# Split scores for the later tiles of an NSA attention, squares of the memory on GpSimd, and two conv halves ahead

## The reference, cut to what matters

```python
def first_block(...):
    h = hybrid_mixer(rmsnorm(x, norms[l, 0]), ...)
    x = x + rmsnorm(h, norms[l, 1])
    h = memory_attention(rmsnorm(x, norms[l, 2]), rmsnorm(mem, mem_norm[l]), ...)
    x = x + rmsnorm(h, norms[l, 3])
    h = swiglu(rmsnorm(x, norms[l, 4]), ...)
    x = x + rmsnorm(h, norms[l, 5])

def hybrid_mixer(h, w_in, w_out, gn_nsa, gn_conv, ...):
    proj = h @ w_in                       # q, three pairs of k and v, gates, conv parts
    ...
    out = g_c[..., 0:1] * o_cmp + g_c[..., 1:2] * o_sel + g_c[..., 2:3] * o_win
    ...
    merged = jnp.concatenate([rmsnorm(o_nsa, gn_nsa), rmsnorm(o_conv, gn_conv)], axis=-1)
    return merged @ w_out
```

## Time and profile before

| | |
|---|---|
| median of 3 runs | 2499.2 us (2498.59 to 2503.46) |
| the profiled execution | 2500.74 us, its span 2498.7 us |
| TensorE busy | 2454.7 us (98%) |
| VectorE, ScalarE, POOL busy | 1578.5, 965.6, 1289.3 us (63%, 39%, 52%) |
| mean granted clock of TensorE | 0.996 |

### The profile page before, as it was taken

One profiled execution on the slowest core, in us unless ns is written; L12 is line 12 of the kernel. 1 busy time (PEld: TensorE's weight loads), 2 busy tenths in 40 slices (PEclk: granted clock), 3 DMA queues, 4 the chain that ended last, 5 costly groups with the idle time before them and its releaser, 6 DMA issues.

```text
span 2498.7 us, 32840 instructions
## 1 busy us (share of the span) xinstructions
PE 2454.7 (98%) x12363; PEld 2074.6 (83%) x12363; DVE 1578.5 (63%) x2572; ACT 965.6 (39%) x1573; POOL 1289.3 (52%) x671
## 2 busy tenths in 40 slices
PE   9999999999999999999999999999999999999998
PEld 6877766877786777788789999999999888888886
DVE  2246244776402735422379897998940699999995
ACT  3256455222323435523333333434333433333333
POOL 3630322444454433144434887766666567666662
PEclk9999999999999999999999999999999999999999
DMA  5320222655433221022223888999998899999992
GB/s 215 118 68 1 68 68 76 202 197 182 152 101 127 76 85 66 32 98 93 101 81 118 297 298 287 356 354 360 358 322 260 296 363 359 364 367 361 367 363 90
DMA packets 212733, 508.90 MB, mean 204 GB/s; under 512 B 18401, under 2 KB 101345, under 8 KB 212193
## 3 DMA queue, kind: packets, MB, share of 16 engines
q1 hardware_dynamic: 123696, 338.22, 38.6%
q0 software_dynamic: 36864, 134.23, 15.1%
q10 hardware_dynamic: 52016, 34.36, 4.4%
HBM read 454.31 MB, written 52.43 MB: 203 GB/s over the span
## 4 chain that ended last, share of the span: by engine, by line
PE 89%; DVE 3%; POOL 3%; ACT 3%; DMA 1%; issue 1%; ACTq 0%; DVEq 0%; SPq 0%
PE bank L2130 73%; PE bank L2682 3%; PE bank_and L2130 3%; POOL weight_split L807 3%; PE bank L2255 3%; PE bank_and L2098 2%; PE bank L2245 1%; ACT weight_split L948 1%; PE bank_and L2230 1%; DMA ring<-weights 1%; PE bank L2230 1%; PE bank L2109 1%; PE bank_and L2495 0%; PE bank L2554 0%; DVE h_split L1424 0%
## 5 line engine op out<-in xcount | busy, mean ns | idle before, releaser
L2130 PE MATMUL bank<-h_split,weight_split 128*128 128x384 f32 (+1 forms) x5568 | 1133.9, 362 | 12.9 <-POOL weight_split L807 4.9
L2130 PEld LDWEIGHTS bank<-h_split,weight_split 128*128 128x128 f32 x5568 | 994.7, 188 | 126.1 <-POOL weight_split L807 11.9
L807 POOL TENSOR_TENSOR weight_split<-ring,weight_split 128x1024 fp32r<-128x1024 f32 x182 | 452.9, 2488 | 758.4 <-ACT weight_split L948 758.2
L2130 PE MATMUL bank<-late_weight_split,weighted_split 128*128 128x512 f32 x2268 | 514.8, 389 | 0.0
L2130 PEld LDWEIGHTS bank<-late_weight_split,weighted_split 128*128 128x128 f32 x2268 | 425.5, 188 | 88.3
L834 POOL DMA_INDIRECT arena<-weights,arena x256 | 314.2, 1228 | 146.1 <-DVE arena L1884 59.6
L823 POOL TENSOR_TENSOR weight_split<-ring,weight_split 128x1024 fp32r<-128x1024 f32 x129 | 310.3, 2406 | 120.8 <-ACT weight_split L1321 120.1
L948 ACT ACTIVATE weight_split<-ring 128x1024 fp32r<-128x1024 f32 x182 | 192.0, 1055 | 292.2 <-PE bank L2130 276.9
L1321 ACT ACTIVATE weight_split<-ring 128x1024 fp32r<-128x1024 f32 x130 | 137.8, 1061 | 390.2 <-PE bank L2130 336.3
L2026 DVE TENSOR_TENSOR arena<-arena 128x384 f32<-128x384 f32 x128 | 224.8, 1756 | 21.3 <-DMA arena<-expert_acts 20.9
L823 POOL TENSOR_TENSOR late_weight_split<-ring,late_weight_split 128x1024 fp32r<-128x1024 f32 x63 | 152.7, 2424 | 102.8 <-ACT late_weight_split L1321 102.2
(11 more groups left out here) (349 smaller groups left out, 2718.3 us busy)
## 6 DMA issues: line engine op xcount, KB each, us to landing
ring<-weights SPq DMA_DIRECT2D x493, 512.0 KB
expert_acts<-arena SPq DMA_DIRECT2D x128, 192.0 KB
gates_spread<-arena ACTq DMA_DIRECT2D x24, 1024.0 KB
arena<-gates_spread SPq DMA_DIRECT2D x96, 256.0 KB
arena<-expert_acts SPq DMA_DIRECT2D x128, 192.0 KB
arena<-weights,arena POOLq DMA_INDIRECT x256
arena<-bias_sel ACTq DMA_DIRECT2D x1, 2048.0 KB, 7.8
arena<-bias_band ACTq DMA_DIRECT2D x1, 2048.0 KB, 7.8
```

The lines of the kernel that those rows point to most:

```text
L807: nc.gpsimd.tensor_tensor(w_split[:, (count - 1) % 2, 1, :], ring[:, n % RING, :], w_split[:, (count - 1) % 2, 0, :], ALU.subtract).then_i ...
L2130: ins = mm(*args, start=start, stop=stop)
```

## The change

The first block only:

- **Scores of the token tiles 2 and 3, window and selected stage.** Each unit's fp32 matmul becomes two fp32r matmuls: one of depth 128, with the query's high part in the rows of its group and its low part in the other half's rows, against the keys' high part in both halves; and one of depth 64, high query by low key (`score_rest`). The new tiles `late_queries_split`, `keys_high_twice` and `keys_low` lie in the space of `h_split`.
- **Who makes the parts.** POOL casts keys and queries and subtracts the keys' low part, after the token values and ahead of w_out's low parts. VectorE copies the keys' high parts to the other half (behind pair 2 and pair 9) and makes the queries' low parts, two behind each of pairs 3 to 6.
- **Memory.** Its DMA is issued by ScalarE at pair 2 of the window stage. POOL squares and adds the chunks behind its attention parts, and TensorE makes one sum matmul of 128x256 instead of 8. ScalarE takes the root behind the selected stage.
- **w_out.** TensorE makes the conv halves of tiles 0 and 1, then turns the merged output, then makes the merged halves of both.
- **Start.** `small` has its own semaphore, const's DMA stands behind x's chunk 2, TensorE waits for const before the second chunk, VectorE before its first evacuation. Six matmuls on zeros instead of eight.

```diff
+            def key_parts(branch):
+                for g in range(2):
+                    nc.gpsimd.tensor_copy(k_twice[half[g], branch, g, :], qk[half[g], 6 + branch, :]).then_inc(k_high, 1)
+                    pool.wait_ge(k_high, 2 * (1 - branch) + g + 1)
+                for g in range(2):
+                    nc.gpsimd.tensor_tensor(k_low[half[g], branch, :], qk[half[g], 6 + branch, :],
+                                            k_twice[half[g], branch, g, :], ALU.subtract).then_inc(k_lowered, 1)
+                    pool.wait_ge(k_lowered, 2 * (1 - branch) + g + 1)
+            def attention_parts():
+                pool.wait_ge(*taken(first["qk"] + 7))
+                pool.wait_ge(proj_done, first["vtok"] + NT)
+                key_parts(1)
+                for n in range(NH):
+                    g, m = n % 2, n // 2
+                    nc.gpsimd.tensor_copy(q_split[half[g], m + 4 * g, :], qk[half[g], m, 2 * P:T]).then_inc(q_high, 1)
+                    pool.wait_ge(q_high, n + 1)
+                key_parts(0)
...
+                if count == tile_of[first["w_out"]]:
+                    attention_parts()
+                    memory_squares()
...
             for k in range(0, KD, 2):
                 act_e.dma_start(xT[:, k, :], x_in[k]).then_inc(x_loaded[k], 16)
-                if k == 0:
+                if k == 2:
                     act_e.dma_start(const[:, :], consts_in).then_inc(consts_in_sem, 16)
...
                 if pair == 2:
+                    act_e.dma_start(memT, mem_in.rearrange("k p m -> p k m")).then_inc(mem_loaded, 16)
                     weight_high(first["w_out"])
...
+            root(2, D, NM)
...
-            act_e.dma_start(memT, mem_in.rearrange("k p m -> p k m")).then_inc(mem_loaded, 16)
...
-            act_e.wait_ge(mem_loaded, 16)
-            norm(2, lambda k: memT[:, k, :], D, NM)
...
+            def query_low(n):
+                g, m = n % 2, n // 2
+                dve.wait_ge(q_high, n + 1)
+                v.tensor_tensor(q_split[half[1 - g], m + 4 * g, :], qk[half[g], m, 2 * P:T],
+                                q_split[half[g], m + 4 * g, :], ALU.subtract).then_inc(q_low, 1)
+            def attention_parts(pair):
+                if pair == 2:
+                    key_in_other_half(1)
+                if 3 <= pair < 7:
+                    query_low(2 * pair - 6)
+                    query_low(2 * pair - 5)
+                if pair == 9:
+                    key_in_other_half(0)
...
+            def score_rest(u, w, q, k):
+                mm(bank[S_BANK[u % 4]][:, 0:w], q, k, start=False, stop=True).then_inc(qk_done, 1)
...
             def nsa_k(i, branch, lo):
+                if t >= 2:
+                    if branch:
+                        pe.wait_ge(q_low, min(i % (2 * NH) + 1, NH))
+                    pe.wait_ge(k_copied, 2 * (2 - branch))
+                    pe.wait_ge(k_lowered, 2 * (2 - branch))
+                    return k_twice[:, branch, g, lo * P:(t + 1) * P]
```

More of the change, by code:

```diff
@@ L786, in add_square, with memory_squares @@
                 nc.gpsimd.tensor_tensor(sum_, before, sq[:, n % 2, :], ALU.add).then_inc(sq_summed, 1)
+            half = [slice(g * HD, (g + 1) * HD) for g in range(2)]
+            def key_parts(branch):
[15 more added lines that the diff above has]
+                key_parts(0)
+            def memory_squares():
+                pool.wait_ge(mem_loaded, 16)
+                nc.gpsimd.tensor_tensor(mem_acc, memT[:, 0, :], memT[:, 0, :], ALU.mult).then_inc(mem_squared, 1)
+                for k in range(1, KD):
+                    pool.wait_ge(mem_squared, 2 * k - 1)
+                    nc.gpsimd.tensor_tensor(mem_sq, memT[:, k, :], memT[:, k, :], ALU.mult).then_inc(mem_squared, 1)
+                    pool.wait_ge(mem_squared, 2 * k)
+                    last = nc.gpsimd.tensor_tensor(mem_acc, mem_acc, mem_sq, ALU.add)
+                    last.then_inc(mem_squared if k < KD - 1 else sq_ready, 1)
             def add_chunks(n, y):
@@ L1575, in _ @@
             late_rstd(0)
+            dve.wait_ge(consts_in_sem, 16)
             for k in range(8):
@@ L2225, in token_major, with score, scores @@
                     release(1)
-            def score(u, w, q, k):
+            def score(u, w, q, k, last=True):
                 if u >= 4:
                     pe.wait_ge(logits_ready, u - 3)
-                mm(bank[S_BANK[u % 4]][:, 0:w], q, k, start=True, stop=True).then_inc(qk_done, 1)
-            def attend(u0, g0, units, per, q, k, blocks, head, vals, before_turn=None, begun=0, busy=(0, 0),
[L2233 to L2237, removed]
+                ins = mm(bank[S_BANK[u % 4]][:, 0:w], q, k, start=True, stop=last)
+                if last:
+                    ins.then_inc(qk_done, 1)
+            def score_rest(u, w, q, k):
+                mm(bank[S_BANK[u % 4]][:, 0:w], q, k, start=False, stop=True).then_inc(qk_done, 1)
+            def attend(u0, g0, units, per, q, k, blocks, head, vals, before_turn=None, begun=0, busy=(0, 0),
+                       after_turn=None, rest=lambda i: None):
+                def scores(pair):
+                    both = [i for i in (2 * pair, 2 * pair + 1) if i >= begun]
+                    for i in both:
+                        score(u0 + i, P * blocks(i), q(i), k(i), last=rest(i) is None)
+                    for i in both:
+                        if rest(i):
+                            score_rest(u0 + i, P * blocks(i), *rest(i))
                 def turn_prob(i):
@@ L2266, in attend @@
                     if pair < units // 2:
-                        scores(2 * pair)
-                        scores(2 * pair + 1)
+                        scores(pair)
                     if pair == 1 and before_turn and not after_turn:
```

89 lines of the change are left out of this document (65 added, 24 removed).

## The result

The changed kernel took 2505.71 us in the median of 22 runs, the kernel before 2500.91 us in as many: a ratio of 1.0035 (95% interval 1.002 to 1.005), slower by 4.8 us where 2.2 us less had been forecast. The single runs say more than the median. Those of before lie between 2498.59 and 2504.76. Those of the changed kernel lie between 2497.91 and 2523.39: three near 2498, nine between 2501 and 2506, eight between 2519 and 2524, and two in between (2508.22 and 2511.48). Their mean granted clock goes with it: 0.995 to 0.997 for the first three, 0.993 to 0.994 for the nine, 0.984 to 0.987 for the eight, 0.992 and 0.989 for the two. The profiled execution is one of the last eight (2522.53, its span 2520.7), so its trace shows what such a run loses.

What follows compares the result with a forecast made beforehand. TensorE, carrying 89% of the chain that ended last, was taken as the bound; start −1.1, window stage +4.5, selected stage −1.1 and w_out −4.5 gave −2.2 on 2499.2: 2497.0 us, range 2490.5 to 2503.5.

Steps and rivals of the forecast that it cites:

- the clock behind pair 7's pause: Window stage: after a 4 us pause TensorE's granted clock falls, adding 1.2 us (0 to 1.7).
- The pause itself: Window stage, VectorE: pair 7's reductions start at 178.0 instead of 173.91, +4.1 us, TensorE idle nearly all of it.
- The casts: POOL, from the window stage's start: 0.9 us for each 512-wide cast, 0.5 at 256.
- case C: Window stage: POOL casts cost 1.4 and 0.75 us, pair 7's reductions come at 181.8 (+7.9); 2501.3 us, chance 0.20.
- Case B: Window stage: VectorE has room, pair 7 stays near 173.91; −7.2 us, 2492.0, chance 0.26.
- Case D: Pair 7 waits as in case C, 64-row rests run one behind the other; +6.6 us, 2505.8, chance 0.12.
- The scores: TensorE: 384-wide pairs take 0.73 us instead of 0.85, rests side by side; window stage −0.8, selected stage −1.1.
- The start: TensorE's first product starts at 10.6 instead of 11.69: −1.1 us (−0.7 to −1.3), and the gain stays.
- w_out: TensorE gains 6.4 us, gives back 2.0 waiting for POOL's low part of tile 2: −4.5.

Runs made afterwards that it cites:

- late lows: The changed kernel with VectorE's query lows two each behind pairs 3, 4, 7 and 8 instead of 3 to 6; 2494.48 us, ratio 0.998.

## Why the prediction was wrong

**The sign and the size fell with one term, the clock behind pair 7's pause.** The prediction took it from the earlier trace rows, where twelve products behind 1.90 us of idling took 4.58, as "1.2 (0 to 1.7)". There the engine had 512-wide products to run, and the clock was back after some 3 us. In the window stage it has small matmuls (64 values wide, transposes of 128, scores of 384), and the fall lasted up to 50 us: +23.4 where +0.4 stood, in a third of the runs; the middle ones are 3 to 8 us above the best. The step assumed that a fall is over once the engine works again, within some 3 us. I had the warning in view: the stage's stream isn't that of the row from which I took the price.

The other terms, as measured, add up to −1.1 + 3.6 (window scores and pause) − 0.8 (selected stage with the memory's sum) − 4.6 = −2.9, that is 2498.0, where the three best runs lie (2497.9 to 2498.4). The forecast without its 1.2 was −3.4. The median is 7.7 us above 2498.0, where 1.2 stood for the clock, and the granted clock of these middle runs is the lower one (0.993 to 0.994). None of them was profiled, so how much of the 7.7 fell in the window stage stays open.

The Trainium skill ("TensorE: Matmul & The Clock Gate", Part 1) says that the array's clock follows how busy it has been of late. The kernel with matmuls behind the pause agrees (spread 1.6 us instead of 25); but busy in the sense of the profile's rows is not enough, as those of 182 to 230 have 4.00 of 4.00 at 0.50.

**The pause itself was right**: +4.4 for +4.1, pair 7's reductions at 178.55, TensorE idle 3.50. Two errors cancelled in it, so the closeness is in part luck. The casts were cheaper than taken (512 wide 0.64 instead of 0.9, and under the 0.77 quoted beside it; 256 wide 0.50 as taken), so case C was far off:

```profile
161.49 1.28 POOL L805 CAST keys_high_twice<-arena 64x512 fp32r<-64x512 f32 x2 [7.53 <-PE bank L2205]
...
165.52 4.02 POOL L819 CAST late_queries_split<-arena 64x256 fp32r<-64x256 f32 x8
```

VectorE's lows waited for more of POOL's work than I had walked: the pairs of them took 2.00 and 1.74. The window output's small operations waited too (128x96 0.48 instead of 0.21, 128x8 0.54 instead of 0.17), while those that read a bank took as long as before (0.42 and 0.69).

**Case B** (no pause) is not what the change does; without the pause, with late lows, it brought −5.7 where B has −7.2. **Case D** named 2505.8, near the median, by another mechanism: the 64-row rests start together (182.54 in the rows below), and C's casts did not come. So the number is no credit to it.

**The scores** gained the forecast sum, 0.12 a pair in the window stage (from one pair's scores to the next 2.83 us instead of 2.95) and 1.1 in the selected stage, but not in the way that was worked out. With late lows (timeline), and the transposes ahead of the earlier trace rows's scores before:

```profile
181.76 0.50 PE L2331 MATMUL bank<-const,arena 128*128 128x128 f32 x3
182.01 0.59 PE L2306 MATMUL bank_and<-keys_high_twice,late_queries_split 128*128 128x384 f32 x2
182.54 0.45 PE L2311 MATMUL bank_and<-keys_low,late_queries_split 64*128 64x384 f32 x2
182.91 0.88 PE L2341 MATMUL bank<-arena 128*128 128x64 f32 x6
```

```profile
181.88 0.50 PE L2245 MATMUL bank<-const,arena 128*128 128x128 f32 x3
```

Scores and rests take 0.90 us of a pair, not 0.73: more than the 0.85 of the fp32 scores, and as much as the prediction gave for rests one behind the other, though they start together. At 512 columns it is 1.07 against 1.05 before. The whole gain is a shorter step from the transposes into the scores (0.25 us instead of 0.43), which no term of the prediction has and whose reason no run shows. That the sum came out is luck.

**The start** was right (first product at 10.44 to 10.61 for 10.6, with the full clock) in the kernels where the clock holds, and lost in the profiled execution. I had looked at six matmuls only as time that no longer delays anything.

**w_out** gave 4.57, and less the memory's sum in front of it (0.3, not 0.47) 4.3 for 4.5, with its wait of 2.00 for 2.0. The fall of the clock behind that wait cost nothing, as another wait was due.

## What to carry to other kernels

Where an engine with a clock that falls when it idles runs a thin stream of small matmuls, price a new pause not by its length but by the stretch of thin work behind it: here 3.5 us of waiting cost up to 27. Look for the crowded few microseconds on the helper engines before adding work there, and put each added operation just ahead of its own consumer; the same operations, two pairs later, turned +4.8 us into −5.7. When single runs of a changed kernel spread far wider than those of the kernel before, read the granted clock by stage before anything else.

## What the runs showed of the hardware

- The granted clock stayed at 0.50 for 50 us while TensorE was busy all the time; a pause of 2.07 us was enough to bring four of twelve runs 12 to 15 us above the best, and in three others did nothing. Behind a pause of 3.5 us half clock lasted 10 us in one trace and over 50 in another.
- Four 512-wide matmuls on constants behind the pause brought the clock back, and the spread of the runs from 25 us to 1.6.
- A POOL cast from fp32 to fp32r of 64x512 takes 0.64 us and one of 64x256 0.50, less than half of the 1.3 of a 512-wide subtraction for the wider one.
- VectorE copies of 64x512 beside POOL took 1.09 us for two beside short operations and 4.09 beside 1024-wide ones.
